# Two weight tiles at once behind each layer norm, in a two-layer decoder trunk in three-term fp32r

## The reference, cut to what matters

```
x  <- LN(ALPHA*x + mixer_0(x))      # norm 0: gMLP + stick-breaking attention
x  <- LN(ALPHA*x + ConvFFN_0(x))    # norm 1
x  <- LN(ALPHA*x + mixer_1(x))      # norm 2: retention, 4 heads
x  <- LN(ALPHA*x + ConvFFN_1(x))    # norm 3, gives y
ConvFFN(x) = (gelu(conv3(x W_gate)) * (x W_val)) W_down
mixer_1, for each of 4 heads: h = x W_in (12 tiles of 128 features), retention, y += o W_out (8 tiles)
```

## Time and profile before

| | before |
|---|---|
| median of 3 runs (lowest to highest) | 2012.45 us (2011.77 to 2016.36) |
| profiled execution, span from first to last instruction | 2007.8 us |
| runs' median less that span | 4.65 us |
| PE busy | 1896.3 us (94%) |
| DVE, ACT, POOL busy | 901.7, 521.6, 149.6 us |

### The profile page before, as it was taken

How to read it: one execution, slowest core, us unless ns; L and a number is a source line. 1 busy time by engine, 2 the same in 40 slices (tenths; PEclk the granted TensorE clock), 3 DMA queues, 4 the chain that set the end, 5 groups by cost and what they waited for, 6 DMA issues and landing times.

```text
span 2007.8 us, 35525 instructions
## 1 busy us (share of the span) xinstructions
PE 1896.3 (94%) x13514; PEld 1653.7 (82%) x13514; DVE 901.7 (45%) x1442; ACT 521.6 (26%) x734; POOL 149.6 (7%) x119
## 2 busy tenths in 40 slices
PE   8898999999799999997998998998998799999996
PEld 8895555558799999996967966966975699999996
DVE  2624333334555345545236237226226655435544
ACT  3322122222322122313222222222222422212213
POOL 0200000000100000002300301301301200000000
PEclk9998999999899999998999999999999999999999
DMA  5446777732123222221224224224333123222231
GB/s 186 161 145 195 248 243 238 239 116 84 42 84 96 92 75 93 95 83 44 88 104 158 85 100 154 89 108 145 95 110 134 58 88 94 95 77 86 87 105 45
DMA packets 83912, 234.16 MB, mean 117 GB/s; under 512 B 9617, under 2 KB 9778, under 8 KB 83490
## 3 DMA queue, kind: packets, MB, share of 16 engines
q1 hardware_dynamic: 83138, 228.19, 34.6%
q0 software_dynamic: 736, 5.48, 0.7%
HBM read 209.84 MB, written 23.80 MB: 116 GB/s over the span
## 4 chain that ended last, share of the span: by engine, by line
PE 84%; DVE 4%; issue 2%; ACT 1%; DVEq 0%; ACTq 0%
PE banks L1169 61%; PE banks L1243 5%; PE banks L1214 3%; PE banks L1442 2%; PE banks L1436 2%; PE banks L1356 2%; PE banks L1428 1%; PE banks L1274 1%; PE banks L1265 1%; PE banks L1284 1%; PE banks L1416 1%; DVE x_lo L942 1%; DVE y L921 1%; PE banks L1458 1%; PE banks L1277 1%
## 5 line engine op out<-in xcount | busy, mean ns | idle before, releaser
L1169 PE MATMUL banks<-x_hi,w_hi 128*128 128x272 f32 x2624 | 550.2, 291 | 44.4 <-DVE x_lo L942 30.3
L1169 PE MATMUL banks<-x_hi,w_lo 128*128 128x272 f32 x2624 | 546.5, 290 | 0.0
L1169 PE MATMUL banks<-x_lo,w_hi 128*128 128x272 f32 x2624 | 546.0, 290 | 0.0
L620 DVE TENSOR_TENSOR w_lo<-w_raw,w_hi 128x1024 fp32r<-128x1024 f32 (+2 forms) x228 | 287.2, 1260 | 516.9 <-ACT w_hi L423 516.9
L423 ACT ACTIVATE w_hi<-w_raw 128x1024 fp32r<-128x1024 f32 (+2 forms) x228 | 238.4, 1046 | 1028.8 <-PE banks L1169 990.4
L1169 PEld LDWEIGHTS banks<-x_hi,w_hi 128*128 128x128 f32 x2624 | 416.0, 190 | 49.8 <-issue 28.9
L1169 PEld LDWEIGHTS banks<-x_lo,w_hi 128*128 128x128 f32 x2624 | 417.0, 191 | 0.0
L1169 PEld LDWEIGHTS banks<-x_hi,w_lo 128*128 128x128 f32 x2624 | 414.1, 191 | 0.0
L1169 PE MATMUL banks<-act_hi,w_lo 128*128 128x272 f32 x704 | 145.3, 288 | 0.0
L1169 PE MATMUL banks<-act_lo,w_hi 128*128 128x272 f32 x704 | 145.2, 288 | 0.0
L1169 PE MATMUL banks<-act_hi,w_hi 128*128 128x272 f32 x704 | 145.2, 287 | 0.0
(11 more groups left out here) (221 smaller groups left out, 1812.0 us busy)
## 6 DMA issues: line engine op xcount, KB each, us to landing
w_raw<-in_w_up SPq DMA_DIRECT2D x88, 512.0 KB, 3.5
kv<-in_kc SPq DMA_DIRECT2D x128, 256.0 KB, 4.1
kv<-in_vc SPq DMA_DIRECT2D x128, 256.0 KB, 3.7
w_raw<-in_w_rin SPq DMA_DIRECT2D x48, 512.0 KB, 3.5
w_raw<-in_w_dn SPq DMA_DIRECT2D x32, 704.0 KB, 4.0
s<-in_s SPq DMA_DIRECT2D x32, 512.0 KB, 7.0
out_ret_s<-s SPq DMA_DIRECT2D x32, 512.0 KB, 2.6
w_raw<-in_w_in_ab SPq DMA_DIRECT2D x20, 512.0 KB, 3.6
```

Source lines behind the costliest of these rows:

```text
L620: V.tensor_tensor(w_lo[:, j, 0:k * P], w_raw[:, j, 0:k * P], w_hi[:, j, 0:k * P].bitcast(F32), ALU.subtract).then_inc(lo_ready, 1)
L1169: last = mm(B[:, 2 * j + half, 0:HN], a[:, j, w], x[:, kt, half * HN:(half + 1) * HN], start=kt == 0 and n == 0, stop=kt == k - 1 and n == 2)
```

## The change

For the products behind norms 0, 1 and 2, the first two tiles are issued together: per contraction block, one wait for `ln_done`, six matmuls of tile 0, six of tile 1. Both tiles' waits (`lo_ready`, `evicted`) stand ahead of the first matmul. The remaining pairs run as before, without the `ln_done` waits. In the retention the joined pair stands in the loop over heads, so that each of the four heads begins with it. The other engines' programs are the same.

```
--- before.py
+++ after.py
@@ -1170,6 +1170,25 @@
                                       start=kt == 0 and n == 0, stop=kt == k - 1 and n == 2)
                 last.then_inc(tile_done, 1)
 
+            def pair_body(k, hi, lo, k_ready):
+                for kt in range(k):
+                    k_ready(kt)
+                    w = slice(kt * P, (kt + 1) * P)
+                    for j in range(2):
+                        for n, (a, x) in enumerate(((w_hi, hi), (w_hi, lo), (w_lo, hi))):
+                            for half in range(2):
+                                last = mm(B[:, 2 * j + half, 0:HN], a[:, j, w], x[:, kt, half * HN:(half + 1) * HN],
+                                          start=kt == 0 and n == 0, stop=kt == k - 1 and n == 2)
+                        if kt == k - 1:
+                            last.then_inc(tile_done, 1)
+
+            def product_behind_norm(base, n, k, hi, lo, k_ready):
+                for j in range(2):
+                    pe.wait_ge(lo_ready, base + j + 1)
+                    pe.wait_ge(evicted[j], base // 2 + 1)
+                pair_body(k, hi, lo, k_ready)
+                product(base + 2, n - 2, k, hi, lo, None)
+
 
             product(U_IN_AB, 8, KD, x_hi, x_lo, lambda kt: pe.wait_ge(x_lo_ready, kt + 1))
 
@@ -1360,7 +1379,11 @@
             def ffn(l):
                 for half in range(2):
                     base = U_FFN[l] + half * (N_UP + N_OUT)
-                    product(base, N_UP, KD, x_hi, x_lo, lambda kt: pe.wait_ge(ln_done, 2 * l * KD + kt + 1))
+                    if half == 0:
+                        product_behind_norm(base, N_UP, KD, x_hi, x_lo,
+                                            lambda kt: pe.wait_ge(ln_done, 2 * l * KD + kt + 1))
+                    else:
+                        product(base, N_UP, KD, x_hi, x_lo, None)
                     product(base + N_UP, N_OUT, KF, act_hi, act_lo,
                             lambda kt: pe.wait_ge(act_ready, (2 * l + half) * KF + kt + 1))
 
@@ -1377,12 +1400,15 @@
             ffn(0)
             norm(1)
             with pe.Fori(0, H_C) as h:
-                with pe.Fori(0, N_RIN // 2) as i:
+                for j in range(2):
+                    pe.wait_ge(lo_ready, h * N_RET + (U_RET + j + 1))
+                    pe.wait_ge(evicted[j], h * (N_RET // 2) + (U_RET // 2 + 1))
+                pair_body(KD, x_hi, x_lo, lambda kt: pe.wait_ge(ln_done, KD + kt + 1))
+                with pe.Fori(1, N_RIN // 2) as i:
                     for j in range(2):
                         pe.wait_ge(lo_ready, h * N_RET + (i * 2 + (U_RET + j + 1)))
                         pe.wait_ge(evicted[j], h * (N_RET // 2) + (i + U_RET // 2 + 1))
-                        tile_body(j, KD, x_hi, x_lo,
-                                  (lambda kt: pe.wait_ge(ln_done, KD + kt + 1)) if j == 0 else None)
+                        tile_body(j, KD, x_hi, x_lo)
 
                 pe.wait_ge(roped, h * 4 + 4)
                 for j in range(2):
```

## The result

The changed kernel takes 2025.41 us, median of 5 runs (2020.95 to 2027.83), against 2012.21 us for the kernel before (5 runs): ratio 1.0065, interval 1.0048 to 1.0081. That is 13 us slower where 5.6 us were forecast, and above the range. The same kernel in a second set of runs: 2023.21 against 2010.66, ratio 1.0053 (1.0036 to 1.0071), 10.7 us slower. Each run lists its own span too: 1.8 us lie around it, not the 4.65 us taken in the prediction, so the sum stands better against the ratio (forecast 1.0028) than against an absolute time.

What follows compares the result with a forecast made beforehand. PE, busy 94% of the span, was taken to bound the kernel. Gains of 11.4 us, head losses of 13.8 and clock losses of 3.2 summed to +5.6 us, 2018.0 us against 2012.45; range 2012.5 to 2023.

Steps and rivals of the forecast that it cites:

- gain behind the norms: Behind norms 0, 1 and 2, tile 2 starts 4.3, 4.3 and 2.8 us sooner; 11.4 us gained in all.
- waits in heads 1 to 3: Each head loses 4.6 us, 2.9 at its start and 1.7 ahead of tile 2; 13.8 us in all.
- clock in heads 1 to 3: PE's clock falls behind the 2.86 us head-start wait in two of three heads, 1.6 us each; 3.2 us.
- The new gaps of 1.7 us behind the pairs are like the 1.81 one: 0: PE's idle gaps ahead of tile 2 cost no clock, judged by a profiled 1.81 us gap; 0 us.
- a sign of its being wrong: Prediction wrong if a head's stall is far from 4.6 us, tile 3 waits, or the clock falls at short gaps.
- the 1.81 us gap: A stretch without PE work in the old profile, granted clock 1.00 at 60 to 62; the lower bound, 0.
- the gap ahead of tile 2: Behind each pair, PE idles about 1.7 us because tile 2's weights may only begin when tile 0 is done.
- 19 slow ones: Norm 0, blocks 0 to 6: 19 half-clock matmuls (4.4 us) fit, so PE reaches block 6 within 0.1 us.
- part of this gain: Behind norm 0 the old clock fell at 524.2 after PE idling; twelve matmuls a block leave no such idling.
- its slack of 0.7 us: Behind norm 0, tile 1's banks are emptied by 534.0 and tile 2 ends at 534.7, so tile 3 doesn't stall.
- the clock that falls in more places: Rival: clock falls at the six 1.7 us gaps too, up to 1.6 us each; up to +17, typically 2025; chance 0.10.
- The clock that holds: Rival: the clock doesn't fall at the head starts, as the skill page's rule has it; +2.4, 2014.9; chance 0.17.

Runs made afterwards that it cites:

- both waits filled: Changed kernel with 12 extra unread matmuls behind each joined pair and 20 ahead of the pair in heads 1 to 3; 2019.03 us, ratio 1.0035.
- the hoisted waits without a pair: Against the changed kernel: no pair anywhere, tiles one after the other, both tiles' waits kept at the head's start; 2022.28 us, ratio 1.0061 against before.

## Why the prediction was wrong

| term | forecast (us) | measured (us) |
|---|---|---|
| gain behind the norms | -11.4 | -9.7 by two profiles' tails (runs: -7.4 and -8.4) |
| clock at the 1.7 us gaps behind the norms | 0 | +1.5 and +0.7 (tails after, 34.5 and 33.6, less 32.95; in the second profile PE was in time behind norm 0 too) |
| waits in heads 1 to 3 | +13.8 | +15.0 (2.9 at a start and 2.1 ahead of tile 2, times 3) |
| clock in heads 1 to 3 | +3.2 | +4.5 (projection, mean of nine heads, 77.23, less 75.74, times 3) |
| sum | +5.6 | +10.5 to +11.3; runs +13.1 and +10.7 |

**The failed step** is "The new gaps of 1.7 us behind the pairs are like the 1.81 one: 0". They aren't free. In the three profiles with the plain pair in the heads, the clock fell behind 4 of 9 such gaps in heads 1 to 3, and behind 5 of 9 of the 2.78 us waits. The prediction had named this as a sign of its being wrong. At 1.5 us a fall, three heads lost 2.5 us at the waits, where the sum had 3.2, and 2.0 us at the gaps, where it had nothing. Two of the 15 such gaps behind norms, over six profiles with the plain pair, fell too, one in each profile of the changed kernel: those tails are 12.22 and 12.25 us, the ones without a fall, and with PE in time, 10.7. The reason given, the 1.81 us gap with its clock at 1.00, was read rightly but doesn't carry over. That gap, too, stands behind dense matmuls, and the clock stayed at 1.00 behind it (58 to 70 us) in all fourteen profiles. So gaps of nearly the same length differ by their place; what makes the difference isn't shown.

**Mis-sized: the gain, and the gap ahead of tile 2.** The gap cost a head 2.1 us for 1.7. Of the gain, 4.3, 4.3 and 2.8 us were 3.2, 4.0 and 2.5 in one profile of the pair behind the norms alone and 3.9, 3.5 and 2.2 in the other. Even where PE was in time for block 6 and no clock fell, a tail took 10.7 us, and the sum has 10.4 (14.69 less 4.3). Where the clock rose late, PE was late too. In norm 0 of the changed kernel PE began at 511.34 and its clock was low until about 517.5 (0.63 in 516 to 518), 6.2 us, where the sum had 4.5. Of "19 slow ones" that fit there came some 27 (6.2 us at 0.225 each), and PE was late at block 6: tile 2 started 528.11 - 511.34 = 16.8 us behind the first block, against 528.7 - 512.86 = 15.8 in the sum. The fall of before's clock was rightly "part of this gain", 1.5 us behind each of norms 0 and 1. That PE had "idled more than half the time" ahead of it doesn't fit the profile: PE was busy for 3.94 of the 6.82 us from 517.41 to 524.23.

**Right.** The place and size of the waits: 2.78 us of idle time for 2.86 at a head's start, 1.74 to 1.77 for 1.7 ahead of tile 2, 5.0 us a head for 4.6 without a fall, and nothing of it given back. Tile 3 behind the norms waits for nothing, as its slack of 0.7 us said. Of the rivals, the clock that falls in more places, at a chance of 0.10, is what happened, but its "typically 2025" is partly luck. It takes some 10 us of clock, six falls at 1.6, and the two profiles of the changed kernel have five and three; a gain 1.7 us too small and waits 1.2 us too long did the rest. The clock that holds, at 0.17, is refuted: it fell behind 5 of the 9 waits of 2.78 us. The Trainium skill ("TensorE: Matmul & The Clock Gate", section "HAM oscillation — how this bites in real kernels") warns of longer idle gaps only, and by it the clock would have stayed up there; the profiles differ.

**Not settled:** why the runs' gain of the pair behind the norms is nearer 8 than the 9.7 us of the tails. The intervals hold both. The extra matmuls behind the pairs didn't help, so a clock that falls there isn't shown to be the cause. Nor is it shown why the clock falls behind one such gap and not behind the next.

## What to carry to other kernels

When two tiles are joined block by block, the wait of the second moves ahead of the first, and the tile after them loses its cover; list what became uncovered and start the second tile some blocks late, by as much as the longest of these waits: here four blocks (3.0 us) took all of the loss away, and with the gain left the kernel was 0.5 to 0.7% faster than before. A new idle gap of TensorE in dense work, even of 1.7 us, is priced as the wait itself and a chance of a fall of the clock, 1.5 us here: in the heads 9 of 18 waits and gaps had one, behind the norms 2 of 15 gaps. A price read at one place needn't hold at another of the same length: the 1.81 us gap cost no clock in fourteen profiles, and the 1.77 us gaps did in 4 of 9. So count falls over several places and profiles before a gap enters a sum as nothing.

## What the runs showed of the hardware

The clock can fall after work has resumed: in the second head TensorE was idle for 1.77 us until 1110.22, and the granted clock was 0.85 in 1110 to 1112, then 0.50. The same gap left it at 1.00 in the third head (1270 to 1274). The nine falls behind waits and gaps in heads 1 to 3 of the three profiles lasted 3.4 us each at 1.2 GHz, 1.7 us of lost work, and made the projection 1.5 us longer (77.26 for 75.74).

Where TensorE came back behind norm 0's 6.8 us wait at 1.2 GHz, the clock rose 2.8 us later (both waits filled) to 6.2 us later (after) in thirteen of the fourteen profiles; before it was 4.5 us. In the fourteenth, the hoisted waits without a pair, it took 13.0 us from 511.03, with six matmuls a block:

```profile
522.00:524.00 2.00, 2.00 (x9) 2.00 (x10) 0.64 (x2) 0.86 (x1) 1.89 (x2) 0.50 0.00 0
```
